# The expert passes of a mixture-of-experts layer: the down products and the scatter of one pass placed inside the next pass

## The reference

```python
logits = hf @ router_w + router_b          # 256 tokens, 32 experts
top_val, top_idx = lax.top_k(logits, 4)
gate = jax.nn.softmax(top_val, axis=-1)
# for each expert e and the tokens that chose it:
u = hf[toks] @ w1[e] + b1[e]               # 1024 -> 2 x 1024
g_, lin = u[:, :D_FF], u[:, D_FF:]
g_ = jnp.minimum(g_, 7.0); lin = jnp.clip(lin, -7.0, 7.0)
y = ((lin + 1.0) * g_ * jax.nn.sigmoid(1.702 * g_)) @ w2[e] + b2[e]
out = segment_sum(y * wts[:, None])        # back to the tokens
```

## Time and profile before

| | |
|---|---|
| median of 3 runs | 1930.34 us (1930.14 to 1932.53) |
| the profiled execution's own time | 1930.87 us |
| its span in the trace | 1929.1 us |
| TensorE busy | 1802.8 us, 93% of the span |
| VectorE, ScalarE, GpSimd busy | 510.2, 252.6, 111.0 us |
| granted TensorE clock, mean | 0.992 |
| expert passes | about 243 to 1187 us of the span |

### The profile page before, as it was taken

How to read it: one execution, slowest core, us unless ns; L and a number is a source line. 1 busy time by engine, 2 the same in 40 slices (tenths; PEclk the granted TensorE clock), 3 DMA queues, 4 the chain that set the end, 5 groups by cost and what they waited for, 6 DMA issues and landing times.

```text
span 1929.1 us, 21701 instructions
## 1 busy us (share of the span) xinstructions
PE 1802.8 (93%) x8583; PEld 1033.3 (54%) x8584; DVE 510.2 (26%) x1032; ACT 252.6 (13%) x519; POOL 111.0 (6%) x148
## 2 busy tenths in 40 slices
PE   6997899999999899899898898989999999899998
PEld 3445733333333233233233234867888888788887
DVE  1237432323222222222132123133110005611000
ACT  1125300110001000000010012013110003211000
POOL 4003600000000000000000001000000000200000
PEclk9998999999999999999999999999999999999999
DMA  9683399979999999999999998430333433444430
GB/s 374 259 264 115 128 405 428 429 305 428 427 429 428 428 429 427 428 429 428 428 428 428 429 428 338 149 113 34 141 131 136 166 135 110 152 153 146 160 131 22
DMA packets 93090, 547.36 MB, mean 284 GB/s; under 512 B 5906, under 2 KB 9186, under 8 KB 65298
## 3 DMA queue, kind: packets, MB, share of 16 engines
q1 hardware_dynamic: 92850, 545.75, 70.2%
q10 hardware_dynamic: 192, 0.92, 0.2%
HBM read 545.60 MB, written 1.05 MB: 283 GB/s over the span
## 4 chain that ended last, share of the span: by engine, by line
PE 62%; DMA 31%; DVE 4%; SPq 1%; issue 1%; ACT 1%; POOL 1%; DVEq 0%; POOLq 0%; ACTq 0%
DMA ring<-in_exp_w 30%; PE ps L1131 20%; PE ps L1230 12%; PE ps L1071 12%; PE ps L753 4%; PE ps L1102 4%; PE ps L943 1%; PE ps L1025 1%; PE ps L1043 1%; PE ps L1265 1%; PE ps L1182 1%; DMA ring<-in_w_in 1%; PE ps L711 1%; DVE arena L2000 1%; SPq L475 0%
## 5 line engine op out<-in xcount | busy, mean ns | idle before, releaser
L1071 PE MATMUL ps<-ring,arena 128*64 128x512 f32 x2112 | 473.9, 595 | 56.5 <-DMA ring<-in_exp_w 56.4
L1131 PE MATMUL ps<-hn,ring 128*128 128x272 f32 (+1 forms) x1536 | 346.5, 388 | 0.0
L1071 PEld LDWEIGHTS ps<-ring,arena 128*64 128x64 f32 x2112 | 148.1, 137 | 362.6 <-issue 240.5
L1131 PEld LDWEIGHTS ps<-hn,ring 128*128 128x128 f32 x1536 | 291.8, 190 | 53.3
L1102 PE MATMUL ps<-arena 128*64 128x512 f32 x1056 | 233.9, 595 | 3.5
L1230 PE MATMUL ps<-arena,ring 128*128 128x272 f32 (+1 forms) x1024 | 228.5, 386 | 1.1 <-DVE arena L1950 1.1
L1230 PEld LDWEIGHTS ps<-arena,ring 128*128 128x128 f32 x1024 | 194.3, 190 | 35.0 <-DVE arena L1950 1.9
L1102 PEld LDWEIGHTS ps<-arena 128*64 128x64 f32 x1056 | 75.2, 137 | 140.9 <-issue 140.6
L1311 ACT ACTIVATE arena<-ps 128x512 f32<-128x512 f32 (+2 forms) x135 | 71.1, 535 | 402.9 <-PE ps L1102 212.2
L1851 DVE TENSOR_SCALAR arena<-ps 128x512 f32<-128x512 f32 x33 | 22.8, 691 | 364.9 <-PE ps L1071 364.9
L1763 DVE TENSOR_SCALAR arena<-arena,rstd 128x64 f32<-128x64 f32 x68 | 18.3, 311 | 304.2 <-PE ps L1071 303.5
(11 more groups left out here) (365 smaller groups left out, 1196.6 us busy)
## 6 DMA issues: line engine op xcount, KB each, us to landing
ring<-in_exp_w SPq DMA_DIRECT2D x128, 2048.0 KB, 24.8
arena<-in_exp_w SPq DMA_DIRECT2D x64, 2048.0 KB, 21.8
ring<-in_mlp_w_up SPq DMA_DIRECT2D x16, 2048.0 KB, 7.5
ring<-in_mlp_w_down SPq DMA_DIRECT2D x16, 2048.0 KB, 7.7
ring<-in_ada_w SPq DMA_DIRECT2D x12, 2048.0 KB, 12.6
ring<-in_sb_w_qkv SPq DMA_DIRECT2D x6, 2048.0 KB, 14.0
ring<-in_w_in SPq DMA_DIRECT2D x5, 2048.0 KB, 9.6
ring<-in_lru_w_in SPq DMA_DIRECT2D x4, 2048.0 KB, 7.9
```

The lines of the kernel that those rows point to most:

```text
L1071: last = mm(bank(2 + part)[64 * h:64 * h + 64, :], lhs, w[:, k % 2, at:at + 512], start=False, stop=(k == C - 1))
L1131: last = mm(bank((n0 + q) % 8)[:, lo:TT], w[:, k, P * q:P * q + P], act[:, k, lo:TT], start=(k == 0), stop=(k == C - 1))
```

## The change

The down products of pass p are no longer at the end of pass p. They run in pass p + 1, between its second and third part of up products (`down`). The scatter of that result is cut in two: its first two products run between the third and the fourth part, the other two behind the gather, where the whole scatter was. Both halves use banks 6 and 7 now, so the second half waits for the additions of the first. VectorE's `add` is cut in the same way: the first half stands ahead of the clamps, the second at the end of the pass. `gathered` moves ahead of `actq`, and on TensorE the turning of `actq` moves to the end of the pass. The bias products no longer wait for `hTe`. In pass 0 the products of `base` go to banks 6, 7, 5, 4, and the turning of `actq` waits until these are copied. ScalarE copies `y` at the start of the next pass. Behind the loop stand one more `down`, the scatter and the additions. The code of SyncE isn't touched: a half of w2 is still released by `w2_parts`, which `down` now signals one pass later.

```diff
-TOKEN_BANKS = (6, 7, 2, 3)
+BASE_BANKS, TOKEN_BANKS = (6, 7, 5, 4), (6, 7, 6, 7)
...
+    def down(p, expert):
+
+        pe.wait_ge(s["aT_ready"], p)
+        for half in range(2):
+            pe.wait_ge(s.w2_loaded[half], expert * 16 + 16)
+            w = m.w2[:, half, :].rearrange("p (k n) -> p k n", n=D)
+            for q in range(4):
+                for h in range(2):
+                    last = mm(bank(5)[64 * h:64 * h + 64, :], m.aT[:, q, 64 * half:64 * half + 64],
+                              w[:, q, 512 * h:512 * h + 512], start=(half == 0 and q == 0),
+                              stop=(half == 1 and q == 3))
+            last.then_inc(s["w2_parts"], 1)
...
-            if first and kk == 1:
-                turn_plan()
+            if kk == 1:
+                if first:
+                    turn_plan()
+                else:
+                    down(p, expert_behind)
+            if kk == 2 and not first:
+                scatter(p, 0)
 
         pe.wait_ge(s["sel_ready"], p + 2)
+        gather()
         if first:
-            gather()
             base()
         else:
-            pe.wait_ge(s["selz_ready"], p)
-            gather()
-            scatter(p, p + 1)
-        pe.wait_ge(s["a_ready"], p + 1)
-        for q in range(4):
-            last = turn(bank(4)[:, P * q:P * q + P], m.actq[:, P * q:P * q + P], ident)
-        last.then_inc(s["a_turned"], 1)
+            scatter(p, 1)
         pe.wait_ge(s["he_ready"], p + 2)
         turn_gathered()
         ...
+        pe.wait_ge(s["a_ready"], p + 1)
+        if first:
+            pe.wait_ge(s["added"], 8)
+        for q in range(4):
+            last = turn(bank(4)[:, P * q:P * q + P], m.actq[:, P * q:P * q + P], ident)
+        last.then_inc(s["a_turned"], 1)
...
     with pe.Fori(1, passes) as p:
-        expert_pass(p, pe.value_load(m.table[0:1, 1, ds(p, 1)], min_val=0, max_val=EXPERTS - 1))
-    pe.wait_ge(s["added"], passes * 4 + 4)
-    scatter(passes, passes)
+        expert_pass(p, expert_of(p), expert_of(p - 1))
+    down(passes, EXPERTS - 1)
+    for t in range(2):
+        scatter(passes, t)
...
+        gathered(p + 1)
         dve.wait_ge(s["dve_chain2"], p + 1)
         dve.wait_ge(s["sg_ready"], p + 1)
         v.tensor_tensor(m.actq.rearrange("p (q n) -> p n q", q=4), m.act.rearrange("p (n q) -> p n q", q=4),
                         m.sg.rearrange("p (n q) -> p n q", q=4), ALU.mult).then_inc(s["a_ready"], 1)
-        gathered(p + 1)
```

More of the change, by code:

```diff
@@ L1014, in base @@
             t, h = n // 2, n % 2
-            if n == 2:
-                pe.wait_ge(s["u_read"], 1)
-            mm(bank(TOKEN_BANKS[n]), m.wT[:, t, :], m.b2[:, 512 * h:512 * h + 512], start=True,
+            mm(bank(BASE_BANKS[n]), m.wT[:, t, :], m.b2[:, 512 * h:512 * h + 512], start=True,
                stop=True).then_inc(s["scattered"], 1)
@@ L1032, in turn_gathered, with scatter @@
         last.then_inc(s["he_turned"], 1)
-    def scatter(p, read):
-        pe.wait_ge(s["y_ready"], p)
-        pe.wait_ge(s["selz_ready"], p)
-        for n in range(4):
-            t, h = n // 2, n % 2
+    def scatter(p, t):
+        if t == 0:
+            pe.wait_ge(s["y_ready"], p)
+            pe.wait_ge(s["selz_ready"], p)
+        for h in range(2):
+            n = 2 * t + h
             rows = slice(64 * h, 64 * h + 64)
-            if n == 2:
-                pe.wait_ge(s["u_read"], read)
+            pe.wait_ge(s["added"], p * 4 + (4 + t * (1 + h)))
             mm(bank(TOKEN_BANKS[n]), m.selz[rows, h, P * t:P * t + P], m.y[rows, :], start=True,
@@ L1051, in program_tensor, with expert_pass @@
     pe.wait_ge(s["split_ready"], 1)
-    def expert_pass(p, expert, first=False):
-        pe.wait_ge(s["hTe_ready"], p + 1)
+    def down(p, expert):
[4 more added lines that the diff above has]
+            for q in range(4):
+                for h in range(2):
+                    last = mm(bank(5)[64 * h:64 * h + 64, :], m.aT[:, q, 64 * half:64 * half + 64],
+                              w[:, q, 512 * h:512 * h + 512], start=(half == 0 and q == 0),
+                              stop=(half == 1 and q == 3))
+            last.then_inc(s["w2_parts"], 1)
+    def expert_pass(p, expert, expert_behind=None):
+        first = expert_behind is None
         if not first:
-            pe.wait_ge(s["added"], p * 4 + 4)
+            pe.wait_ge(s["u_read"], p)
         for part in range(2):
@@ L1061, in expert_pass @@
                    m.b1parts[:, part, 512 * h:512 * h + 512], start=True, stop=False)
+        pe.wait_ge(s["hTe_ready"], p + 1)
         for kk in range(4):
@@ L1094, in expert_pass, with expert_of @@
         last.then_inc(s["selt_done"], 1)
[L1096 to L1107, removed]
+        pe.wait_ge(s["a_ready"], p + 1)
[4 more added lines that the diff above has]
+        last.then_inc(s["a_turned"], 1)
+    def expert_of(p):
+        return pe.value_load(m.table[0:1, 1, ds(p, 1)], min_val=0, max_val=EXPERTS - 1)
+    expert_pass(0, 0)
     passes = pe.value_load(m.passes[0:1, 0:1], min_val=EXPERTS, max_val=MAX_PASSES)
     with pe.Fori(1, passes) as p:
-        expert_pass(p, pe.value_load(m.table[0:1, 1, ds(p, 1)], min_val=0, max_val=EXPERTS - 1))
-    pe.wait_ge(s["added"], passes * 4 + 4)
-    scatter(passes, passes)
+        expert_pass(p, expert_of(p), expert_of(p - 1))
+    down(passes, EXPERTS - 1)
+    for t in range(2):
+        scatter(passes, t)
     pe.wait_ge(s["added"], passes * 4 + 8)
@@ L1419, in program_scalar, with place_down @@
     nc.scalar.preload_act_table(ACT.Sigmoid)
+    def place_down(p):
+        act.wait_ge(s["w2_parts"], p * 2)
+        copy(m.y, bank(5), "y_ready")
     def expert_pass(p):
@@ L1424, in expert_pass @@
         f(m.sg, m.g, ACT.Sigmoid, scale=1.702).then_inc(s["sg_ready"], 1)
-        act.wait_ge(s["a_turned"], p + 1)
-        copy(m.aT, bank(4).rearrange("p (q n) -> p q n", q=4), "aT_ready")
         act.wait_ge(s["selt_done"], p + 1)
@@ L1429, in expert_pass @@
         copy(m.selz[64:P, 1, :], bank(0)[64:P, 0:T], "selz_ready")
-        act.wait_ge(s["w2_parts"], p * 2 + 2)
-        copy(m.y, bank(5), "y_ready")
+        act.wait_ge(s["a_turned"], p + 1)
+        copy(m.aT, bank(4).rearrange("p (q n) -> p q n", q=4), "aT_ready")
     expert_pass(0)
@@ L1436, in program_scalar @@
     with act.Fori(1, passes) as p:
+        place_down(p)
         expert_pass(p)
+    place_down(passes)
     def squares(number, signal, base):
@@ L1774, in turned_gather, with add @@
         v.tensor_copy(m.hTe, bank(1).rearrange("p (j n) -> p j n", j=4)).then_inc(s["hTe_ready"], 1)
-    def add(p):
-        for n in range(4):
-            t, h = n // 2, n % 2
+    def add(p, t):
+        for h in range(2):
+            n = 2 * t + h
             dve.wait_ge(s["scattered"], p * 4 + (n + 1))
@@ L1788, in begin @@
             dve.wait_ge(s["scattered"], n + 1)
-            v.tensor_copy(m.acc[:, t, 512 * h:512 * h + 512], bank(TOKEN_BANKS[n])).then_inc(s["added"], 2)
+            v.tensor_copy(m.acc[:, t, 512 * h:512 * h + 512], bank(BASE_BANKS[n])).then_inc(s["added"], 2)
     select(0)
@@ L1849, in expert_pass @@
                         ALU.is_equal, ALU.mult).then_inc(s["selw_ready"], 1)
+        if not first:
+            add(p, 0)
         dve.wait_ge(s["w1_parts"], p * 4 + 4)
@@ L1858, in expert_pass @@
                         m.sg.rearrange("p (n q) -> p n q", q=4), ALU.mult).then_inc(s["a_ready"], 1)
-        gathered(p + 1)
         if first:
             begin()
-        else:
-            add(p)
         dve.wait_ge(s["he_turned"], p + 2)
         turned_gather()
+        if not first:
+            add(p, 1)
     expert_pass(0, first=True)
@@ L1870, in program_vector @@
         expert_pass(p)
-    add(passes)
+    for t in range(2):
+        add(passes, t)
     for n in range(C):
```

1 line of the change is left out of this document (removed).

## The result

| | before | after |
|---|---|---|
| median, us | 1931.43 (1930.14 to 1932.72, 4 runs) | 1977.53 (1973.60 to 1979.14, 4 runs) |
| profiled execution, us | 1930.87 | 1973.60 |
| its span, us | 1929.1 | 1971.8 |

The change makes the kernel slower: ratio 1.0228, 95% interval 1.0206 to 1.0249, that is 44 us by the ratio and 46 by the two medians. The forecast was 1959.3, range 1952.5 to 1968.0: the sign and most of the mechanism are right, the size is a third too small, and the time lies outside the range.

The account below looks back on a forecast made before the run. The prediction took the sequence of loads, six a pass, to bound the kernel. Terms 6.6 + 11.8 + 5.6 + 0.7 = 24.7 us, plus 4.3 mid-stream, gave 29.0 us more: 1959.3 us, range 1952.5 to 1968.

Parts of the forecast that it names:

- What bounds the kernel: Expert passes: six loads of 4.90 us set 29.38 us a pass; TensorE, 93% busy, has 3.15 us to spare.
- The release of w2: Halves of w2 are freed only after two up parts and half a down of the next pass, holding later w1 loads.
- start: Passes 0 and 1: expert 1's first w2 half lands at 284.8 instead of 278.2, +6.6 us.
- repeated expert: Expert 5 to 6: first w2 halves land 54.1 us apart instead of 42.3, +11.8 us.
- end: Last pass: from the last first w2 half's landing to the end of down, 16.3 us instead of 10.7, +5.6 us.
- The extra reads of the table by TensorE's sequencer: TensorE's loop: costed at nothing behind queued up products; without that cover each is below half a microsecond.
- the mid-stream term: Ordinary passes: w2 load issued 2.5 us ahead leaves a hole of 0.16 us, 27 times, +4.3 us.
- rival 2: Mid-stream w2 loads: a large hole of 0.35 to 1.0 us a pass, 1964 to 1982 us; chance 0.12.
- rival 1: Mid-stream w2 loads: no hole, the fixed part runs beside the load in front; 1955.0 us; chance 0.28.
- rival 3: TensorE becomes the bound by an uncounted wait, passes longer than 29.4 us; 1974 us at 30 us a pass; chance 0.04.
- rival 4: Late w2 doesn't break the load stream; only the end counts, less 2.4 us at the repeated expert; 1934.2 us; chance 0.03.
- rival 5: Faster through the first w1 slot freed early at the repeated expert: 2.4 us less, 1927.9 us; chance 0.02.

Follow-up runs that it names:

- the turned loop: Changed kernel with TensorE's loop cut behind the fourth up part, so the table reads stand behind queued up products: 1975.70 us, ratio 1.0215.
- the filled kernel: The turned loop plus three unread products between bias products and first up part in each pass but the first: 1977.31 us, ratio 1.0225.
- both edits: Changed kernel with the loop cut behind the fourth up part and down products between first and second up part: 1951.15 us, ratio 1.0103.
- both edits with the filling: The kernel with both edits plus three unread products ahead of the first up part in each pass but the first: 1953.35 us, ratio 1.0106.

## Why the prediction was wrong in size and right in kind

**What bounds the kernel.** Right: loads in sequence, and not TensorE at 93%. The old order with a late w2 alone loses 21 us with TensorE's program untouched, and with the down products one up part earlier the landings of mid-stream are back at 29.38 us a pass.

**The release of w2, start, repeated expert, end.** Right in mechanism and place. The forecast of the late release alone came out at 20.9 us for 21, partly by luck: start and repeated expert are 19.1 of it, and the rest comes behind the last down, where no term stood. In the changed kernel start and repeated expert were 2.2 and 1.6 us short. For the start, TensorE's way from gather to the first up products was 1.6 us longer than forecast, with 2.1 us of reads in it, and the lower clock cost another 1.7; against them stood a gather that came 0.9 us earlier and a load of 7.5 us for 7.7. For the repeated expert it is the reads.

**Failed: "The extra reads of the table by TensorE's sequencer I cost at nothing, since some 40 instructions stand queued behind the up products there".** They stood behind a wait for VectorE, and the sequencer took the reads only when that was over: 1.4 us with nothing queued at each of 32 boundaries. The forecast had one read without cover below half a microsecond; with its checks it is 0.7. They cost 2.6 us at the repeated expert by the turned loop, partly offset there by a tail that was 0.5 shorter than forecast in each of two passes. In mid-stream they cost nothing by themselves, since the load comes later.

**Failed, and the larger miss: the mid-stream term, "I take 0.16, half-way to 0.32".** A load with 2.5 us of lead takes the full 7.7 us: 813.7 in the changed kernel, 829.6 with a lead of 1.0. The whole 0.32 was due (the middle one of 25 passes is 29.71 us, for 29.38), and by landings it is due 29 times: 9.3 of the 13.3 us measured. I had taken the middle because "2.5 is close to 2.8", which is no argument; the only row for a short lead, the 7.7 us on an empty queue, asked for 0.32. The rest, 4.0 us in the profile, are single passes that are longer. The upper bound of 1.0 us a pass held (a mean of 0.44 in the changed kernel behind the repeated expert, 0.6 in the filled one), but rival 2, which was this case with a chance of 0.12, got too little. That its range, 1964 to 1982, holds the measured time is partly luck: 0.46 us in each of 27 passes, with the forecast's other terms, gives some 1967, and the others were short too.

**Not foreseen: the late single loads.** A loop with a lead of only 2.5 us pays for each load that is late; with five loads queued the kernel before shows 29.37 to 29.39 us in each pass from expert 12 on, so the same lateness, if it is there, is hidden. Shown at full clock in the filled kernel (9.5 for 7.7), and in the changed one at 633.5 (9.6). What makes such a load late is open.

**Not foreseen: the granted clock.** It fell at the start of pass 1 and cost 1.7 us there, and twice more in the passes, behind 386 and 652 us. That it has to do with the idle stretches is shown by filling them; which stretch brings it down is not. What it costs in mid-stream is nothing with a long lead. In the changed kernel the lead tells what it cost: behind each of the two stretches the next load is issued 2.2 to 2.3 us ahead of the landing before it, for 2.5, so 0.2 us each. The late load of the pass of 31.74 us came first, at 633.5, and the clock fell at 652. The remaining 1.5 us behind the passes weren't followed by an experiment, nor were the 3.9 us between the profiled execution and the median; the three runs above the profiled one have mean granted clocks of 0.982 to 0.985 for its 0.987, which would fit, but isn't shown as the cause.

**Rivals 1, 3, 4 and 5** fell: the hole exists, TensorE is not the bound (it still waits 1.24 us for the second w1 part in ordinary passes of mid-stream), the stream has its new holes, and nothing became faster. None of the variants run beats the kernel before; the best, both edits, is 1.0% slower (ratio 1.0103).

## What to carry to other kernels

Where a stream of loads sets the time, ask of each moved step when it frees its buffer, and compare the time from issue to landing on an empty queue with what is still queued at that moment; if the lead is shorter than the fixed part, count the whole difference in every turn of the loop, and more for the occasional late load. A busy share of 93% on the compute engine is no reason to rearrange it. Reads by an engine's sequencer cost nothing here where queued work that waits for nothing stood ahead of them, and their full time where a wait did.

## What the runs showed of the hardware

- A load of 2.10 MB costs 4.90 us in a full queue and 7.5 to 8.0 us from issue on an empty one, once 8.5 (expert 1 with the down products moved). With a lead of 2.5 us it is still 7.7; now and then 8.1 to 9.6 in such a place, and once 10.1 in the turned loop. With leads of 3.5 us and more the first half of w2 landed 4.9 us behind the load ahead, but for one of 5.3 (both edits with the filling, expert 7, lead 3.9).
- TensorE's granted clock went to 1.2 GHz behind an idle stretch of 2.45 us that followed turnings and short products, but not behind each such stretch (694.92), and also behind two pieces of 1.27 and 0.70 us (556.17); it stayed at 2.4 GHz in all passes once the three short products were put in, 1.5 us of work. In the kernel before, waits of 1.24 us among up products never brought it down in the passes.
- Two reads of a small table by TensorE's sequencer, with their checks, took 1.4 us when nothing was queued.
